# Loading each expert of the later groups of three in one transfer of 3 MiB, instead of two of 2 and 1 MiB

## The chip, the cores and the metric

The kernel runs on one core of one Trainium2 chip. The metric is the device time of one execution in microseconds (us). PE is the matrix engine, ACT the scalar engine, DVE the vector engine, POOL the general one, and SP the engine that only waits and issues DMA transfers here.

## What is computed

Two layers of a small diffusion transformer on 256 tokens of width 1024. Layer 0 mixes tokens by attention and a state space model, layer 1 by a long convolution (hyena). After the mixer each layer has a mixture of experts: 64 experts with a hidden width of 256, of which every token uses six, and a shared expert.

```python
def expert_block(args):
    toks, w, e = args
    xb = xf[toks]
    hid = jax.nn.silu(xb @ w_gate[e]) * (xb @ w_up[e])
    return (hid @ w_down[e]) * w[:, None].astype(xb.dtype)
...
routed = jnp.zeros_like(xf).at[row_tok].add(ys.reshape(n_rows, Dm))
shared = (jax.nn.silu(xf @ sh_gate) * (xf @ sh_up)) @ sh_down
return (routed + shared).reshape(B, L, Dm)
```

Everything is in 32-bit floats. One expert is 3 MiB: gate and up 2 MiB, down 1 MiB. All 64 are read in each layer, 192 MiB, whatever the routing.

## The kernel before

**Groups.** The 64 experts of a layer are worked through in 22 groups (`NG`). The first two are pairs, the other 20 are triples, numbered t = 0 to 19 (group n = t + 2). A triple puts its biggest expert in 64 rows of the array and the two others in 32 each. The order of the experts is computed at run time (`order`), so SP reads each expert's number into a register before it asks for its weights.

**The ring of weights.** On chip there are six slots of 3 MiB (`wring`, `RING = 6`), so triple t lies where triple t-2 lay. In memory an expert is one row per partition, gate and up (16 KiB) followed by down (8 KiB), and the slot has the same form. `half_loads` (L517) asks for one half of each expert of a triple, SP's queue having, for each t: three gate-and-up halves, each after a wait on `gu_mm` for group t-2 (its gate-and-up products are done), then three down halves, each after a wait on `dn_mm` for group t-2 (its down products are done). They count on `w_gu0` or `w_gu1`, and `w_dn0` or `w_dn1`, by the parity of t. All of these transfers are in one hardware queue and are served in order by the same 16 DMA engines.

**A group on PE** (`moe_pe`, the loop from L1091): wait for `w_gu` of its triple; gate-and-up products (64 matmuls of 512 columns); products that scatter the rows of the group before (`filler`), and those that pick and turn the rows of the group after; the turn of the hidden values; wait for `w_dn`; down products (32 matmuls), which count `dn_mm` up. `triple_loads(t, li)` is the number of expert loads that must have landed on one of the semaphores. In the trace all these matmuls have line 678, the turns of hidden values and of rows line 984, and every load has line 451. The last group has no next rows to pick and turn.

**After a stage.** When the last group is down, its rows are scattered, the residual is added, and layer 1's norm and projection follow on PE. The projection's weights (`hy_w_in`) are asked for after `dn_mm` of the last but one group.

Of the kernel before, what the change touches and what calls it, by code (L numbers as in the profile page):

```python
# [35 lines left out]
RING, FIRST_SLOT, SHARED = 6, 3, 2  # L36
# [3 lines left out]
PAIRS = STATIC // 2  # L40
NG = PAIRS + (NE - STATIC) // 3
BIG = STATIC + NG - PAIRS
FIRST, GROUP = 4, 12
SECOND, FILL_AT, LATER = 9, 11, 16
CTAB_STEPS = 24
# [54 lines left out]
def group_of(c):  # L100
    return c // 2 if c < STATIC else PAIRS + (c - STATIC) // 3
# [20 lines left out]
def program(nc, A):  # L122
# [8 lines left out]
    with ExitStack() as ctx:  # L131
        sems = {}

        def sem(name):
            if name not in sems:
                sems[name] = ctx.enter_context(nc.semaphore(name))
            return sems[name]
# [120 lines left out]
        wring = at(m1, RING * WEXP).rearrange("p (b n) -> p b n", b=RING)  # L258
# [40 lines left out]
        loads, ahead = rt_at(34, NE), rt_at(35, NE)  # L299
# [15 lines left out]
        def slot_of(e):  # L315
            return (e + FIRST_SLOT) % RING

        def triple_loads(t, li):

            fixed = li + 1 if t % 2 == 0 else 0  # L320
            return 3 * (li * len(range(t % 2, NG - PAIRS, 2)) + t // 2 + 1) - fixed
# [127 lines left out]
        def _(sp):  # L449
# [58 lines left out]
            def moe_loads(li):  # L508
                sp.wait_ge(sem("x_mixed"), KD * (li + 1))
                load(rw, A["router_w"][li], "rw_in")  # L510
                load(rt_at(0, NE), A["router_b"][li:li + 1].broadcast_to([P, NE]), "rw_in")
                load(at(r_mc, NMCST), A["mcst"], "rw_in")
                first_experts(li, (3, 4))

                def expert_at(c):
                    return sp.value_load(order[0:1, c:c + 1], min_val=0, max_val=NE - 1)
                GUW = 2 * KD * FF  # L517

                def half_loads(columns, experts, t, down):
                    part, name = (slice(GUW, WEXP), f"w_dn{t % 2}") if down else (slice(0, GUW), f"w_gu{t % 2}")  # L520
                    for c in columns:
                        if c - RING >= 0:
                            sp.wait_ge(sem("dn_mm" if down else "gu_mm"), li * NG + group_of(c - RING) + 1)
                        elif down:
                            sp.wait_ge(sem("sh_down"), li + 1)
                        else:
                            sp.wait_ge(sem("sh_gu"), 2 * (li + 1))
                        load(wring[:, slot_of(c), part], A["w_experts"][li, experts[c]][:, part], name)
                sp.wait_ge(sem("tables_ready"), TABLES * li + 1)
                first = {c: expert_at(c) for c in range(FIXED, STATIC + 6)}  # L530
                half_loads((5, 6), first, 0, False)
                half_loads((7,), first, 1, False)
                half_loads((5, 6), first, 0, True)
                half_loads((7,), first, 1, True)
                half_loads((8, 9), first, 1, False)
                half_loads((8, 9), first, 1, True)
                for t in range(2, NG - PAIRS):
                    triple = range(STATIC + 3 * t, STATIC + 3 * t + 3)
                    experts = {c: expert_at(c) for c in triple}
                    half_loads(triple, experts, t, False)  # L540
                    half_loads(triple, experts, t, True)
                if li == 0:
                    sp.wait_ge(sem("hscr_out"), 16)
                    sp.wait_ge(sem("dn_mm"), NG - 1)
                    for n in range(3):
                        load(hyw[:, n], A["hy_w_in"][HYP[n]], f"hyw_in{n}")
                sp.wait_ge(sem("dn_mm"), (li + 1) * NG)
                sp.wait_ge(sem("hscr_out"), 16 * (li + 1))

                def more(s, i):  # L550
                    sp.wait_ge(sem(f"ov_d{li}"), i * OVD + OVD * NE * (s - 1) + 1)
                    e = sp.value_load(order[0:1, bass.ds(i, 1)], min_val=0, max_val=NE - 1)
                    sp.dma_start(wring[:, 0], A["w_experts"][li, e]).then_inc(sem(f"ov_w{li}"), 16)
                overflow(li, sp, more)
# [121 lines left out]
        def _(pe):  # L676
# [55 lines left out]
            for i in range(FIRST):  # L732
                pe.wait_ge(sem(f"ada_c{i}"), 16)
                for k in range(KD):
                    g, a = k % 4, 2 * (GROUP - 1 - i)
                    last = mm(ps[32 * g:32 * g + 2 * GROUP, 4, :], scz[:, k, a:a + 2 * GROUP], ada_first[i][:, k],
                              i == 0 and k < 4, i == FIRST - 1 and k >= 4, skip=True)
                last.then_inc(sem("ada_mm"), 1)
            pe.wait_ge(sem("adrow_ready"), 1)
            for j in range(4):  # L740
                last = mm(ps[:, 3, 2 * FIRST * j:2 * FIRST * (j + 1)], adrow[:, j * P:(j + 1) * P], cst("fold")[:, 0:2 * FIRST], True, True)
# [3 lines left out]
            for k in range(KD):  # L745
                pe.wait_ge(sem("h_ctx"), k + 1)
                pe.wait_ge(sem("h_x"), k + 1)
                last = mm(ps[:, 0, :], w_in[:, k, QL:QL + KVL], hT[:, k], k == 0, k == KD - 1)
            last.then_inc(sem("proj_mm"), 1)
            for k in range(KD):  # L750
                g = k % 4
                last = mm(ps[32 * g:32 * g + ROPE, 1, :], w_in[:, k, QL + KVL:UOFF], hT[:, k], k < 4, k >= 4, skip=True)
            last.then_inc(sem("proj_mm"), 1)
            for i in range(2):
                for k in range(KD):
                    last = mm(ps[:, 2, i * L:(i + 1) * L], w_in[:, k, i * P:(i + 1) * P], hT[:, k, L:2 * L], k == 0, k == KD - 1)
# [16 lines left out]
            for i in range(2):  # L773
                last = mm(ps[:, 2, 0:L], ones, sql[0][:, i * L:(i + 1) * L], i == 0, i == 1)
# [11 lines left out]
            for h in range(HEADS):  # L786
                for k in range(2):
                    last = mm(ps[0:QKH, 3 + h // 2, (h % 2) * L:(h % 2 + 1) * L], w_uq[:, k, h * QKH:(h + 1) * QKH], ql[:, k], k == 0, k == 1)
# [30 lines left out]
            for h in (0, 2, 1, 3, 4, 6, 5, 7):  # L819
                if h % 4 == 0:  # L820
                    pe.wait_ge(sem("sq_head"), h // 2 + 2)
                last = head_sum(h, 0, L, sqq[:, h // 2, (h % 2) * L:(h % 2 + 1) * L], False)
# [20 lines left out]
            for h in (0, 2, 4, 6, 1, 3, 5, 7):  # L843
                last = over_features(ps[0:QKH, turning[h // 2], (h % 2) * L:(h % 2 + 1) * L], h, 2 * L, L, False)
# [79 lines left out]
            for n in range(2 * HEADS):  # L924
# [5 lines left out]
                for k in range(4):  # L930
                    last = pe.transpose(ps[:, 2 + n % 2, k * P:(k + 1) * P], prob[:, n % 3, k * P:(k + 1) * P], ident)  # L931
# [20 lines left out]
            for p in range(4):  # L952
                last = s5_outputs(p)
# [9 lines left out]
            for t in range(T5):  # L963
                last = pe.transpose(ps[:, 5 + t // 4, (t % 4) * P:(t % 4 + 1) * P], ys[:, t].rearrange("p g c -> p (g c)"), ident)  # L964
# [5 lines left out]
            for j in range(4):  # L970
                for k in range(4):
                    last = mm(ps[:, 5 + j // 2, (j % 2) * L:(j % 2 + 1) * L], glu_w[:, k, j * P:(j + 1) * P], zT[:, k], k == 0, k == 3)
# [8 lines left out]
            def moe_pe(li):  # L981
# [109 lines left out]
                for n in range(NG):  # L1091
                    t = n - PAIRS
                    if t < 0:
                        pe.wait_ge(sem(f"w_pair{n}"), 16 * (2, 3)[n] * (li + 1))
                    else:
                        pe.wait_ge(sem(f"w_gu{t % 2}"), 16 * triple_loads(t, li))
                    pe.wait_ge(sem("xt_act"), li * NG + n + 1)
                    pe.wait_ge(sem("xt_dve"), li * NG + n + 1)
                    if n >= 1:
                        pe.wait_ge(sem("h_done"), li * NG + n)  # L1100
                    gate_up_of(n).then_inc(sem("gu_mm"), 1)
                    if n == 0:
                        pe.wait_ge(sem("sh_hidden"), li + 1)
                    else:
                        pe.wait_ge(sem("oh_ready"), li * NG + n)
                        pe.wait_ge(sem("y_dve"), 2 * (li * NG + n))
                    filler(n, range(0, 4))
                    if n + 1 < NG:
                        pick_rows(n + 1)
                    filler(n, range(4, 6))  # L1110
                    if n < NSETS:
                        pe.wait_ge(sem("tables_ready"), TABLES * li + 2 + n)
                    pe.wait_ge(sem("h_done"), li * NG + n + 1)
                    for f in range(2):
                        last = turn(ps[:, HT, f * P:(f + 1) * P], hh[:, f * P:(f + 1) * P], ident, f == 0)
                    last.then_inc(sem("ht_mm"), 1)
                    if n + 1 < NG:
                        turn_rows(n + 1)
                    filler(n, range(6, KD)).then_inc(sem("sc_mm" if n >= 1 else "sh_down"), 1)
                    pe.wait_ge(sem("hT_ready"), li * NG + n + 1)  # L1120
                    if n + 1 < NG:
                        pe.wait_ge(sem("xt_act"), li * NG + n + 2)
                        pe.wait_ge(sem("xt_dve"), li * NG + n + 2)
                    if t >= 0:
                        pe.wait_ge(sem(f"w_dn{t % 2}"), 16 * triple_loads(t, li))
                    down_of(n).then_inc(sem("dn_mm"), 1)
                    if n + 1 < NSETS:
                        find_tokens(n + 1)
# [1117 lines left out]
```

## Time and profile before

| | us |
|---|---|
| median of three runs | 1501.29 |
| lowest and highest run | 1499.29, 1504.4 |
| the profiled execution's own time | 1497.9 |
| its span from first to last instruction | 1496.1 |
| PE busy | 1320.8 (88%) |
| expert stage of layer 0, from the first groups to the last down | about 320 to 786 |
| expert stage of layer 1 | about 1011 to 1479 |

The profile shows one execution. Its time is the span and 1.8 us around it. Section 1 of the page has the busy time of each engine, section 2 the same in 40 equal slices of 37.4 us with what the DMA engines moved, section 4 the chain of work that ended last (54% PE, 37% DMA), section 6 the transfers by size. A weight load that PE waits for ends a stretch of idle time; the timeline shows that time in brackets with what released it.

### The profile page before, as it was taken

The page shows a single profiled execution, that of the slowest core. Times are in us where ns is not written, and L with a number is a line of the kernel's source. Part 1 is how long each engine was busy: PE and PEld are TensorE (multiplying, and loading weights), DVE is VectorE, ACT ScalarE, POOL GpSimd, SP SyncE. Part 2 cuts the span into 40 slices and gives each one's busy share as a digit, 9 for nine tenths or more (in the row PEclk, how much of TensorE's full clock was granted, in tenths as well). Part 3 has the DMA queues.
Part 4 walks back from the last instruction along what each step waited for, and adds up shares of the span by engine and source line. Part 5 has one row for each costly group of instructions (what it writes and reads, how often), then busy time and mean ns, then how long its engine had stood idle before and what let it go on. Part 6 is the DMA issues. An engine that isn't in the chain of part 4 may idle for free.

```text
span 1496.1 us, 22046 instructions
## 1 busy us (share of the span) xinstructions
PE 1320.8 (88%) x9056; PEld 685.7 (46%) x9056; DVE 634.9 (42%) x1170; ACT 298.5 (20%) x501; POOL 66.7 (4%) x116
## 2 busy tenths in 40 slices
PE   4998778899998888897887999999999888898895
PEld 1444326764444333333436776875444333343342
DVE  5997733254433223222224788453433222322322
ACT  2236232311111111111112114031111111111110
POOL 0000681000000000000000000000000000000000
PEclk9999889999999999999997999989999999999998
DMA  9672963958999999999997870767999999999993
GB/s 381 238 180 71 188 262 126 396 219 322 420 423 421 423 423 423 423 423 423 422 423 230 303 297 29 303 245 267 380 424 424 421 425 421 421 424 423 422 423 130
DMA packets 59800, 502.79 MB, mean 336 GB/s; under 512 B 10348, under 2 KB 17260, under 8 KB 20588
## 3 DMA queue, kind: packets, MB, share of 16 engines
q1 hardware_dynamic: 59148, 499.19, 83.9%
q8 instruction: 76, 1.25, 0.3%
q10 hardware_dynamic: 544, 2.10, 0.3%
q14 instruction: 32, 0.26, 0.0%
HBM read 496.57 MB, written 4.69 MB: 335 GB/s over the span
## 4 chain that ended last, share of the span: by engine, by line
PE 54%; DMA 37%; DVE 4%; issue 2%; ACT 2%; SPq 1%; DVEq 0%; ACTq 0%
PE ps L678 50%; DMA arena<-in_w_experts 34%; DMA arena<-in_ada_w 3%; PE ps L407 2%; ACT arena L1278 1%; SPq L451 1%; PE ps L984 1%; DVE arena L1885 1%; PE ps L723 0%; ACT L1278 0%; DVE arena L1718 0%; PE ps L931 0%; DVE arena L1719 0%; DVE arena L1742 0%; DVE arena L1716 0%
## 5 line engine op out<-in xcount | busy, mean ns | idle before, releaser
L678 PE MATMUL ps<-arena 128*32 128x512 f32 (+12 forms) x8236 | 1235.1, 497 | 151.8 <-DMA arena<-in_w_experts 78.4
L678 PEld LDWEIGHTS ps<-arena 128*32 128x32 f32 (+6 forms) x8236 | 622.5, 132 | 749.2 <-issue 543.6
L1278 ACT ACTIVATE arena<-ps 128x512 f32<-128x512 f32 (+7 forms) x303 | 167.5, 553 | 928.9 <-PE ps L678 817.5
L1278 ACT ACTIVATE arena<-arena 128x256 f32<-128x256 f32 (+8 forms) x138 | 93.6, 700 | 171.5 <-DVE arena L1940 61.1
L1924 DVE SCALAR_TENSOR_TENSOR arena<-arena,ps 128x256 f32<-128x256 f32 x44 | 21.2, 481 | 234.1 <-ACT arena L1278 234.1
L1938 DVE CAST arena<-ps 128x512 bf16<-128x512 f32 x44 | 30.4, 692 | 175.0 <-PE ps L678 175.0
L1881 DVE COPY arena<-ps 128x512 f32<-128x512 f32 x44 | 30.4, 692 | 172.7 <-PE ps L678 172.7
L1914 DVE TENSOR_TENSOR arena<-arena 128x1024 bf16<-128x1024 f32 x44 | 53.9, 1226 | 39.5 <-ACT arena L1278 39.2
L1940 DVE TENSOR_TENSOR arena<-ps,arena 128x1024 f32<-128x1024 f32 x44 | 53.9, 1225 | 1.5
L668 POOL MEMSET arena<- 128x1 f32 x2 | 0.2, 101 | 1215.1 <-PE ps L984 1215.1
L984 PE MATMUL ps<-arena 128*128 128x128 f32 x352 | 52.8, 273 | 0.0
L407 PE MATMUL ps<-arena 128*24 128x512 f32 x256 | 35.6, 651 | 8.4 <-DMA arena<-in_ada_w 8.4
L1885 DVE COPY arena<-ps 128x512 f32<-128x512 f32 x44 | 30.4, 692 | 26.1 <-PE ps L984 26.1
L984 PEld LDWEIGHTS ps<-arena 128*128 128x128 f32 x352 | 41.4, 141 | 0.0
L1278 ACT ACT_TABLE_LOAD x15 | 19.2, 1283 | 67.7 <-PE ps L964 24.9
L1736 DVE TENSOR_REDUCE arena<-ps 128x1 f32<-128x512 f32 x16 | 11.1, 692 | 27.9 <-PE ps L678 27.7
L2055 DVE SCALAR_TENSOR_TENSOR arena<-arena 128x512 f32<-128x512 f32 x28 | 21.1, 752 | 1.2 <-DMA arena<-in_ada_w 0.3
L1932 DVE COPY arena<-ps 128x256 f32<-128x256 f32 x44 | 18.4, 419 | 5.2 <-PE ps L984 5.2
L1278 ACT ACTIVATE arena<-ps,arena 128x512 f32<-128x512 f32 (+3 forms) x29 | 17.0, 585 | 15.7 <-PE ps L678 14.9
L407 PEld LDWEIGHTS ps<-arena 128*24 128x24 f32 x256 | 6.1, 105 | 28.5 <-DMA arena<-in_ada_w 15.3
L931 PE MATMUL ps<-arena 128*128 128x128 f32 x64 | 10.7, 293 | 5.7 <-DVE arena L1742 5.7
L625 POOL TENSOR_TENSOR arena<-arena 128x64 f32<-128x64 f32 (+4 forms) x21 | 12.8, 608 | 60.3 <-ACT arena L1278 58.7
(225 smaller groups left out, 479.6 us busy)
## 6 DMA issues: line engine op xcount, KB each, us to landing
arena<-in_w_experts SPq DMA_DIRECT2D x118, 2048.0 KB, 28.0
arena<-in_w_experts SPq DMA_DIRECT2D x118, 1024.0 KB, 27.4
arena<-in_ada_w SPq DMA_DIRECT2D x40, 1024.0 KB, 6.5
arena<-in_w_experts SPq DMA_DIRECT2D x10, 3072.0 KB, 18.7
arena<-in_hy_w_in SPq DMA_DIRECT2D x6, 2048.0 KB, 12.0
arena<-in_ada_w SPq DMA_DIRECT2D x4, 2048.0 KB, 22.1
arena<-in_w_shared SPq DMA_DIRECT2D x2, 3072.0 KB, 10.5
arena<-in_hy_w_out SPq DMA_DIRECT2D x1, 4096.0 KB, 12.5
```

The source lines that it names most:

```text
L407: last = pe.matmul(ps[32 * k:32 * k + 2 * GROUP, 7, :], scz[:, 4 * half + k, a:a + 2 * GROUP], ada_half(i, half)[:, k], start=i == first a ...
L678: return pe.matmul(out, lhsT, rhs, start=start, stop=stop, skip_group_check=skip)
L984: return mm(out, in_, one, True, True) if first else pe.transpose(out, in_, one)
L1278: return act.activation(out, in_, func, **kw)
L1881: dve.tensor_copy(picked[:, 512:], ps[:, DN + 1, :]).then_inc(sem("picked_dve"), 1)
L1885: dve.tensor_copy(xgT[:, 4:8].rearrange("p k t -> p (k t)"), ps[:, DN + 1, :]).then_inc(sem("xt_dve"), 1)
L1914: tt(yb[:, 2], yr, yb[:, 1], SU).then_inc(sem("y_dve"), 1)
L1924: stt(hh, sg, wtab[:, n:n + 1], ps[:, GU, FF:2 * FF], M, M).then_inc(sem("h_done"), 1)
L1932: dve.tensor_copy(hT2.rearrange("p f t -> p (f t)"), ps[:, HT, 0:2 * P]).then_inc(sem("hT_ready"), 1)
L1938: ch(dve.tensor_copy(yb[:, 0, 0:512], ps[:, DN, :]))
L1940: tt(yr, ps[:, DN:DN + 2, :].rearrange("p b n -> p (b n)"), yb[:, 0], SU).then_inc(sem("y_dve"), 1)
L2055: ins = ts(ada_sums[n], w, c, None, M) if half == 0 and k == 0 else stt(ada_sums[n], w, c, ada_sums[n], M, AD)
```

## The change

`whole(t)` is true for t = 8 to 18. For such a triple SP waits, per expert, for the down products of group t-2, and then asks for all 3 MiB in one transfer, which counts on `w_gu`. PE waits for it ahead of gate-and-up, and no longer ahead of down. Triples 0 to 7 and 19 are loaded in halves as before. `down_loads` is the new count for `w_dn`. Nothing else differs.

```diff
+TRIPLES = NG - PAIRS
...
+        def whole(t):
+
+            return 8 <= t < TRIPLES - 1
+
+        def down_loads(t, li):
+
+            def loads(last):
+                return sum(0 if whole(i) else 2 if i == 0 else 3 for i in range(t % 2, last + 1, 2))
+            return li * loads(TRIPLES - 1) + loads(t)
+
...
                     experts = {c: expert_at(c) for c in triple}
+                    if whole(t):
+                        for c in triple:
+                            sp.wait_ge(sem("dn_mm"), li * NG + group_of(c - RING) + 1)
+                            load(wring[:, slot_of(c)], A["w_experts"][li, experts[c]], f"w_gu{t % 2}")
+                        continue
                     half_loads(triple, experts, t, False)
                     half_loads(triple, experts, t, True)
...
-                    if t >= 0:
-                        pe.wait_ge(sem(f"w_dn{t % 2}"), 16 * triple_loads(t, li))
+                    if t >= 0 and not whole(t):
+                        pe.wait_ge(sem(f"w_dn{t % 2}"), 16 * down_loads(t, li))
                     down_of(n).then_inc(sem("dn_mm"), 1)
```

## Rows read from the trace of the kernel before

**Rows 1.** The page's 40 slices: PE, DMA busy in tenths, GB/s.
```profile
PE   4998778899998888897887999999999888898895
...
DMA  9672963958999999999997870767999999999993
GB/s 381 238 180 71 188 262 126 396 219 322 420 423 421 423 423 423 423 423 423 422 423 230 303 297 29 303 245 267 380 424 424 421 425 421 421 424 423 422 423 130
```
**Rows 2.** Waits of PE, 460 to 780 us: us in total, times, longest.
```profile
PE ps L678 <- DMA arena<-in_w_experts: 39.6, 14, 4.9
```
**Rows 3.** PE timeline (start, us, what), the turn in two groups before DMA binds.
```profile
452.54 0.27 PE L984 MATMUL ps<-arena 128*128 128x128 f32 x1
...
471.01 0.27 PE L984 MATMUL ps<-arena 128*128 128x128 f32 x1
```
**Rows 4.** Windows: stretch, length, busy of each engine, clock, DMA share, GB/s.
```profile
500.00:740.00 240.00, 205.70 (x1497) 87.76 (x1490) 65.13 (x106) 34.65 (x54) 0.00 (x0) 0.96 1.01 423
...
948.00:972.00 24.00, 24.00 (x112) 20.96 (x112) 6.33 (x15) 1.62 (x4) 0.00 (x0) 1.00 1.00 429
```
**Rows 5.** PE timeline, the last three groups of layer 0 (t = 17 to 19).
```profile
727.74 12.82 PE L678 MATMUL ps<-arena 128*32 128x512 f32 x92 [2.06 <-DMA arena<-in_w_experts]
...
742.77 3.64 PE L678 MATMUL ps<-arena 128*32 128x512 f32 x32 [0.33 <-DVE arena L1885]
749.98 14.52 PE L678 MATMUL ps<-arena 128*32 128x512 f32 x92 [3.57 <-DMA arena<-in_w_experts]
...
766.71 3.64 PE L678 MATMUL ps<-arena 128*32 128x512 f32 x32 [0.33 <-DVE arena L1885]
772.23 9.39 PE L678 MATMUL ps<-arena 128*32 128x512 f32 x84 [1.89 <-DMA arena<-in_w_experts]
...
781.57 4.39 PE L678 MATMUL ps<-arena 128*128 128x256 bf16 x38
```
**Rows 6.** Windows of one gate-and-up each; the clock stands third from the end.
```profile
749.98:758.80 8.82, 8.82 (x65) 2.42 (x66) 1.05 (x2) 0.00 (x0) 0.00 (x0) 0.81 1.03 432
727.74:734.87 7.13, 7.13 (x65) 2.06 (x66) 1.49 (x2) 1.04 (x1) 0.00 (x0) 1.00 1.04 432
1171.37:1181.40 10.03, 10.03 (x66) 2.44 (x67) 1.49 (x2) 0.00 (x0) 0.00 (x0) 0.71 1.02 425
```
**Rows 7.** PE timeline, layer 1: t = 6, then t = 19.
```profile
1171.35 15.72 PE L678 MATMUL ps<-arena 128*32 128x512 f32 x92 [3.11 <-DMA arena<-in_w_experts]
...
1189.28 3.64 PE L678 MATMUL ps<-arena 128*32 128x512 f32 x32 [0.33 <-DVE arena L1885]
...
1463.66 11.08 PE L678 MATMUL ps<-arena 128*32 128x512 f32 x84 [4.08 <-DMA arena<-in_w_experts]
...
1474.69 4.39 PE L678 MATMUL ps<-arena 128*128 128x256 bf16 x38
```
**Rows 8.** The chain of waits: PE's end, then SP's first issue.
```profile
556.86 0.02 issue
...
557.02 0.34 SPq L451
```
**Rows 9.** SP's issue on an empty queue, and windows right after it.
```profile
944.93 0.33 SPq L451 DMA_DIRECT2D arena<-in_w_shared  x1
...
944.90:945.85 0.95, 0.95 (x6) 0.84 (x5) 0.88 (x3) 0.00 (x0) 0.00 (x0) 1.00 0.00 0
...
945.85:949.85 4.00, 4.00 (x20) 3.48 (x20) 3.72 (x9) 0.00 (x0) 0.00 (x0) 1.00 1.06 381
```
**Rows 10.** PE timeline, layer 0: t = 6, then t = 7 and 8.
```profile
480.13 14.52 PE L678 MATMUL ps<-arena 128*32 128x512 f32 x92 [3.11 <-DMA arena<-in_w_experts]
...
502.21 12.83 PE L678 MATMUL ps<-arena 128*32 128x512 f32 x92 [1.72 <-DMA arena<-in_w_experts]
...
517.25 3.64 PE L678 MATMUL ps<-arena 128*32 128x512 f32 x32 [0.33 <-DVE arena L1885]
525.79 4.64 PE L678 MATMUL ps<-arena 128*32 128x512 f32 x28 [4.90 <-DMA arena<-in_w_experts]
```

## The prediction

> **What bounds the kernel now.** I read the page's forty slices first [rows 1]. From the 11th slice to the 21st and from the 30th to the 39th, in the two expert stages, the DMA engines are busy throughout and move 420 to 425 GB/s; PE is busy for 80 to 90%. The reader is to see that the stream from memory doesn't pause, so it is the likely bound. PE's waits say the same: between 460 and 780 us PE waits 14 times for expert weights, 39.6 us in all [rows 2]. The PE timeline prices both sides. Unhindered, a group of three repeats every 18.5 us (452.54 to 471.01) [rows 3]. A triple of experts is 9 MiB = 9.44 MB, and 9.44 MB at the 423 GB/s of 500 to 740 us [rows 4] takes 22.3 us. Starts of gate-and-up 22.25 us apart (727.74, 749.98, 772.23) [rows 5] are exactly that. So from the seventh triple on (t = 6) DMA sets the pace, and PE idles 1.9 to 3.6 us a group.
>
> PE's own time from the start of gate-and-up to the end of down, W, has two common values: 727.74 to 746.41 = 18.7 us, and 749.98 to 770.35 = 20.4 us [rows 5]. The first gate-and-up ran at granted clock 1.00 in 7.13 us, the second at 0.81 in 8.82 us, a part of it at 1.2 GHz [rows 6]. The slower one follows the longer idle time (3.57 against 2.06 us). In layer 1 one took 10.03 us at 0.71 [rows 6]; W was 1171.35 to 1192.92 = 21.6 us [rows 7].
>
> **How much slack the order of requests leaves now.** Triple t takes the slots of t-2. Its gate-and-up halves (6 MiB) are asked for when gate-and-up of t-2 is through, its down halves (3 MiB) when down of t-2 is. PE starts t as soon as the gate-and-up halves land, 7.4 us (3.15 MB at 423) before the down halves do. The down request comes W = 20 us after that start, and the transfer is due 22.3 + 7.4 + 14.9 us after it; so the queue is tens of microseconds deep and never runs dry.
>
> **What the change does to it, for t = 8 to 18 (eleven triples, 33 experts a layer).**
>
> (a) Transfers. 66 transfers of 2 and 1 MiB become 33 of 3 MiB; the bytes are the same. SP issues 33 fewer at 0.33 us each, hidden under its waits. The pure 3 MiB stream at 948 to 972 us ran at 429 GB/s against 423 [rows 4]: 22.0 us a triple for 22.3, a gain of 0.31 us, times 11 = 3.4 us a layer. It counts only while the queue is continuous. I take it as measured; the bounds are 0 and twice that.
>
> (b) PE now needs all 9 MiB before gate-and-up. At t = 8 that shifts PE by 7.4 us relative to the stream, once; the bytes behind it aren't delayed. The shift costs nothing in the middle, as the stream sets the pace, but it must be repaid at the last triple. In layer 0 the halves of t = 19 landed at 772.2 [rows 5]. Their 6.29 MB take 14.9 us, so the down halves of t = 18 were in at 757.3. A whole t = 18 lands then, less the gain of (a): 753.9. PE runs it for W = 20.4 (it is an even one, which follow the long idle time) and reaches t = 19 at 774.3 instead of 772.2: +2.1 us. In layer 1: 1463.6 - 14.9 - 3.4 + 20.4 = 1465.7 against 1463.66 [rows 7]: +2.1 us. The last group then starts without idle time ahead of it. In layer 0 it took 772.23 to 785.96 = 13.7 us, in layer 1 1463.66 to 1479.08 = 15.4 [rows 5, 7], so layer 1 gets back 1.7. Sum of (a) and (b): +2.1 + 2.1 - 1.7 = **+2.5 us**. If W of t = 18 is 18.7 in both layers it is 3.4 less, -0.9. The new end of either layer is the PE chain that follows, so it passes on whole.
>
> (c) The moved request. The load of t+2 is asked for only at the end of down of t: start of t + W. Now start of t is the landing of the whole triple, and the stream has just t+1 left, 22.0 us. From the end of a group on PE to the start of SP's issue is 0.16 us (556.86 to 557.02) [rows 8]. An issue at 944.93 on an empty queue moved nothing before 945.85, and the next 4 us ran at 381 GB/s [rows 9] instead of 429, a loss of 0.45 us. The new transfer therefore runs at full value W + 0.16 + 0.95 + 0.45 = W + 1.55 us after the landing: 20.25, 21.95 or 23.15 us for the three W. Against 22.0: 1.75 us in hand, none, or 1.15 short. The cover that hid the request is gone in every second group.
> - t = 8 waits for its whole triple: in layer 0 from down's end at 520.9 [rows 10] to about 533 (the gate-and-up halves landed at 525.8, plus 7.4), 12 us idle. No row shows a group after so long an idle time; the nearest is the 21.6 of layer 1, and 18.7 is the other end. I take 21.6: t = 10 is 1.15 late.
> - Four more even groups are targets (t = 12 to 18). Their sources run slow, and the rows show both kinds, 8.8 and 10.0 us [rows 6]; the 8.8 has more rows. I count a third at 1.15 and two thirds at 0.1: 0.45 x 4 = 1.8 us.
> - The 16 DMA engines don't finish together. Now the interval of starts is 22.25 but now and then 23.6 (502.21 to 525.79) [rows 10]; the mean over t = 6 to 19 is (772.23 - 480.13)/13 = 22.47 [rows 5, 10]. A deep queue lets undisturbed engines run ahead; a shallow one doesn't, so a delay on any engine counts. Its price isn't shown; bounds 0 and, if the 0.22 doubles, 2.4 us a layer; I take 1.1, the middle, as nothing draws it to an end.
> Sum of (c): 1.15 + 1.8 + 1.1 = 4.05 a layer, **+8.1 us** (bounds 0 and 2 x (5 x 1.15 + 2.4) = 16.3).
>
> Nothing else is queued behind SP's moved wait: its next entries were the down requests with the same wait. PE loses eleven waits a layer on `w_dn`, none of which was ever last. The hyena weights of layer 1 are asked for after down of t = 18, at 774 instead of 770, while the stream is busy to about 776 with t = 19: hidden.
>
> **A rule that speaks for the change.** The measured gain per transfer removed is 0.31/3 = 0.1 us [rows 4]. The Trainium skill, "DMA: Bandwidth & Descriptors", section "Anatomy of one DMA", gives a fixed cost of about 2.0 us per DMA beside the movement. Charged to each of the 66 transfers saved, that would be an estimate of 132 us gained; the trace disagrees, since a queue with the next transfer waiting runs at 423 GB/s. The same fixed cost says what a dry queue pays, and there the trace has about 1.55 us.
>
> **Rivals.**
> 1. *Stall-free.* The queue stays continuous after all: W + 1.55 never exceeds what is left. For it: 21.95 against 22.0, and DMA engines that run behind have more left. Against: no margin. Time: 1497.9 + 2.5 = 1500.4, -0.9 to +4 around it; within 0.3%.
> 2. *Clock feedback, slower still.* A late landing lengthens PE's idle time, the next gate-and-up falls to 0.71 of the clock, W = 21.6 or more, and the next request is later. It decides as soon as idle time ahead of even groups passes some 4 us. For it: the 21.6 of layer 1 [rows 7]. Against: after 4.90 us idle at 525.8 W was 20.1. Time: the bound, 1497.9 + 2.5 + 16.3 = 1516.7.
> 3. *Faster.* The 3 MiB stream reaches 440 GB/s, as single slices of the trace do for a moment; 21.45 us a triple, gain 0.86 x 11 x 2 = 19 us instead of 6.8, 12 us more: 1488 if requests still kept up. But W + 1.1 = 21.5 already exceeds 21.45, so it can't be whole; with half the triples held at 22 half of the 12 us is left, 1494. (The Trainium skill's fixed cost above is this rival at its extreme.) Against it: 429 in the one row there is.
> 4. *Not what it says.* Before t = 8 the stream already sets the pace, so the change does bite; a semaphore count that made PE wait for t+2 would deadlock and not shift time. No chance of its own.
>
> **How the numbers follow.** Forecast: 1497.9 + 2.5 + 8.1 = 1508.5 us for an execution like the profiled one (span 1496.1 and 1.8 around it). That execution is 3.4 under the median of 1501.29, so for the median: 1501.3 + 10.6 = 1511.9 us. Chances: forecast 0.67, stall-free 0.22, feedback 0.07, faster 0.04. A measurement tells 0.3%, 4.5 us, from no change. The forecast's own low end (+5) lies just over that bound, so slower 0.73, same 0.23, faster 0.04. Range: from the stall-free case's low end, 1501.3 - 0.9 = 1500, to 1501.3 + 2.5 + 16.3 = 1520, and 3 more for the spread of the runs (1504.4 against 1501.3): 1523.
>
> **What would show it.** Step (a): GB/s of a stretch in t = 9 to 18, 429 if the queue is continuous. Step (b): t = 8 of each layer starts 12 us after the down before it; t = 19 starts with no idle time for DMA ahead of it, and the last group takes 13.7 us in both layers. Step (c): start intervals that alternate, about 22.0 and 22.3 to 23.1, DMA share under 1.00 in short windows after each whole landing, slow gate-and-ups in every second group. The prediction is wrong if intervals stay at 22.0 throughout (rival 1), or if PE's gate-and-up stays at 7.1 us, which would leave 1.75 us in hand everywhere.

## The result, and the profile after

The changed kernel takes 1523.45 us (median, 1522.54 to 1524.94) against 1500.29 us (the three runs of the table before and a fourth): a ratio of 1.0157, 95% interval 1.0136 to 1.0177, 23.2 us slower. The forecast had the sign and the mechanism, but less than half of the size, and the range ended 0.45 us short.

The page's slices, which answer to [rows 1], and its transfers by size (count, KB, median us to landing):

```profile
PE   4998778999999788888987999989999877898886
DMA  9572964958999999999996871767999999999993
GB/s 379 222 184 70 208 234 158 384 206 321 422 424 422 426 389 394 430 404 407 410 398 215 313 287 45 298 241 286 381 422 423 424 429 398 406 403 388 429 407 124
...
arena<-in_w_experts SPq DMA_DIRECT2D x76, 3072.0 KB, 19.1
arena<-in_w_experts SPq DMA_DIRECT2D x52, 2048.0 KB, 20.0
arena<-in_w_experts SPq DMA_DIRECT2D x52, 1024.0 KB, 18.8
...
arena<-in_w_shared SPq DMA_DIRECT2D x2, 3072.0 KB, 10.6
```

In the expert stage of layer 0 (11th to 21st slice) the stream is as before up to the 14th slice. From the 15th on, where the whole triples begin, it moves 389 to 410 GB/s, with one slice of 430; in layer 1, from the 34th slice on, it moves 388 to 407, with one of 429. So the stream now pauses. The last line matters below.

The PE timeline of layer 0 (start, us, what, the idle time before it and its releaser) from t = 8 to 13, and the end of the layer, which answer to [rows 5, 10]:

```profile
537.09 15.08 PE L694 MATMUL ps<-arena 128*32 128x512 f32 x92 [12.35 <-DMA arena<-in_w_experts]
559.05 12.83 PE L694 MATMUL ps<-arena 128*32 128x512 f32 x92 [1.14 <-DMA arena<-in_w_experts]
583.70 15.67 PE L694 MATMUL ps<-arena 128*32 128x512 f32 x92 [6.08 <-DMA arena<-in_w_experts]
601.46 3.64 PE L694 MATMUL ps<-arena 128*32 128x512 f32 x32 [0.22 <-DVE arena L1901]
605.77 12.82 PE L694 MATMUL ps<-arena 128*32 128x512 f32 x92 [0.66 <-DMA arena<-in_w_experts]
630.86 14.32 PE L694 MATMUL ps<-arena 128*32 128x512 f32 x92 [6.53 <-DMA arena<-in_w_experts]
653.04 3.27 PE L694 MATMUL ps<-arena 128*32 128x512 f32 x20 [2.12 <-DMA arena<-in_w_experts]
...
769.67 14.52 PE L694 MATMUL ps<-arena 128*32 128x512 f32 x92 [4.06 <-DMA arena<-in_w_experts]
786.29 12.83 PE L694 MATMUL ps<-arena 128*32 128x512 f32 x116 [0.22 <-DVE arena L1901]
799.07 4.39 PE L694 MATMUL ps<-arena 128*128 128x256 bf16 x38
```

t = 8 starts after 12.35 us idle, as foreseen. Then the distances between starts alternate: 21.96, 24.65, 22.07, 25.09, 22.18 us. At the end t = 19 begins in the same row as the down products of t = 18 (786.29, 116 matmuls), without idle time.

The whole difference by stage, from the starts of gate-and-up in the two timelines, in us:

| stage | layer 0: before, after | layer 1: before, after | sum of differences |
|---|---|---|---|
| t = 7 to t = 8 | 23.6, 31.0 | 22.2, 29.5 | +14.7 |
| t = 8 to t = 18 | 224.2, 232.6 | 225.1, 233.4 | +16.7 |
| t = 18 to t = 19 | 22.3, 20.1 | 22.8, 18.4 | -6.6 |
| last group | 13.7, 13.7 | 15.4, 13.7 | -1.7 |

That is 23.1 us, the difference of the medians. The two profiled executions (1497.9 and 1524.0) are 3 us further apart, and that part lies outside the stages.

**One dry restart**, end of down of t = 10 (605.10) to the start of t = 12. SP's row, then windows with clock, DMA share and GB/s at the end:

```profile
605.30 1.37 SPq L462 DMA_DIRECT2D arena<-in_w_experts  x3
```

```profile
603.00:604.00 1.00, 1.00 (x12) 0.31 (x8) 0.00 (x0) 0.00 (x0) 0.00 (x0) 1.00 0.24 98
604.00:605.00 1.00, 1.00 (x12) 0.16 (x4) 0.00 (x0) 0.00 (x0) 0.00 (x0) 1.00 0.12 49
605.00:606.20 1.20, 0.54 (x8) 0.16 (x8) 1.00 (x2) 0.60 (x1) 0.00 (x0) 1.00 0.00 0
606.30:608.30 2.00, 2.00 (x24) 0.57 (x20) 0.88 (x2) 1.06 (x1) 0.00 (x0) 1.00 1.06 332
608.30:610.30 2.00, 2.00 (x24) 0.64 (x20) 1.43 (x2) 0.00 (x0) 0.00 (x0) 1.00 0.91 393
610.30:626.00 15.70, 13.81 (x100) 6.65 (x92) 4.27 (x8) 2.18 (x4) 0.00 (x0) 1.00 1.00 430
```

A window counts a packet of 24 KB, 0.9 us long, where it starts, so after 603 few DMA engines begin another (0.24, then 0.12). By the packets in the trace 12 of the 16 have done their part of t = 11 by 603.9, the last at 605.3, and its landing is seen at 605.7, when PE starts it (605.77). SP asks at 605.30; nothing moves before 606.2; full rate is back after 610. t = 12 starts at 630.86, which is 25.8 us after the end of down. 9.44 MB at 430 GB/s are 21.95, so this restart costs 3.8 us beside the bytes. The same span is there at every even triple, t = 10 to 18 in both layers: 25.6 to 26.4 us, mean 26.0, so a restart costs 4.0 us on average. For instance in layer 1, down of t = 14 to the start of t = 16, and of t = 16 to t = 18:

```profile
1396.88 3.64 PE L694 MATMUL ps<-arena 128*32 128x512 f32 x32 [0.22 <-DVE arena L1901]
...
1426.47 14.17 PE L694 MATMUL ps<-arena 128*32 128x512 f32 x92 [6.84 <-DMA arena<-in_w_experts]
...
1442.73 3.64 PE L694 MATMUL ps<-arena 128*32 128x512 f32 x32 [0.22 <-DVE arena L1901]
...
1472.17 12.83 PE L694 MATMUL ps<-arena 128*32 128x512 f32 x92 [3.35 <-DMA arena<-in_w_experts]
```

1400.52 to 1426.47 is 25.95, 1446.37 to 1472.17 is 25.8. So the rule with which I went into the experiments (theory A; I took the span as 25.9): on a chain of triples two apart, start to start takes W + 25.9 us if the queue ran dry, and the pair can't be faster than the stream's 43.9. It is dry once W exceeds 18.0. W of the even groups was 19.8 to 21.6, mean 20.6.

### The profile page after: what moved, and what is told of

Same layout as the page of the kernel before. It is cut to its first block, busy times and chain, and to the rows that moved or that the text cites. A ratio compares the mean times of both kernels' runs of the same rounds, so it can differ in the third digit from the quotient of the medians.

```text
span 1522.1 us, 21826 instructions
## 1 busy us (share of the span) xinstructions
PE 1326.7 (87%) x9056; PEld 687.7 (45%) x9056; DVE 635.6 (42%) x1170; ACT 298.6 (20%) x501; POOL 66.8 (4%) x116
## 4 chain that ended last, share of the span: by engine, by line
PE 63%; DMA 28%; DVE 5%; issue 2%; ACT 1%; SPq 1%; DVEq 0%; ACTq 0%
PE ps L694 58%; DMA arena<-in_w_experts 24%; DMA arena<-in_ada_w 3%; PE ps L418 2%; PE ps L1000 2%; SPq L462 1%; DVE arena L1901 1%; ACT arena L1294 1%; PE ps L947 0%; PE ps L739 0%; DVE arena L1734 0%; DMA arena<-in_mcst 0%; DVE arena L1735 0%; ACT L1294 0%; DVE arena L1732 0%
## 5 line engine op out<-in xcount | busy, mean ns | idle before, releaser
L1000 PEld LDWEIGHTS ps<-arena 128*128 128x128 f32 x352 | 41.4, 141 | 0.0
L1948 DVE COPY arena<-ps 128x256 f32<-128x256 f32 x44 | 18.4, 419 | 5.3 <-PE ps L1000 5.3
L418 PEld LDWEIGHTS ps<-arena 128*24 128x24 f32 x256 | 6.4, 106 | 26.4 <-issue 13.9
L947 PEld LDWEIGHTS ps<-arena 128*128 128x128 f32 x64 | 8.2, 151 | 16.1 <-DVE arena L1758 11.0
## 6 DMA issues: line engine op xcount, KB each, us to landing
arena<-in_hy_w_in SPq DMA_DIRECT2D x6, 2048.0 KB, 10.1
arena<-in_ada_w SPq DMA_DIRECT2D x4, 2048.0 KB, 22.2
```

The source lines that it names most:

```text
L418: last = pe.matmul(ps[32 * k:32 * k + 2 * GROUP, 7, :], scz[:, 4 * half + k, a:a + 2 * GROUP], ada_half(i, half)[:, k], start=i == first a ...
L1000: return mm(out, in_, one, True, True) if first else pe.transpose(out, in_, one)
```

## The experiments

Each runs beside the kernel before, whose median was 1498.4 to 1499.6 us. "Halves" are the transfers of 2 and 1 MiB.

**1. Late requests alone** (in the kernel before):

```diff
-                            sp.wait_ge(sem("dn_mm" if down else "gu_mm"), ...)
+                            sp.wait_ge(sem("dn_mm" if down or 8 <= t < 19 else "gu_mm"), ...)
```

> Halves of 2 and 1 MiB as in the kernel before, PE's waits as before; only the gate-and-up halves of t = 8 to 18 are asked for after the down products of t-2 too. Theory A (a late request hurts only together with PE's late start, because then the queue holds no more than one triple, 22 us, while the request comes W = 18.6 to 20.4 us after the start and takes nearly 4 us to be at full rate): here PE starts 7.4 us earlier than the queue's backlog ends, about 29.7 us are queued, so no stall: within 2 us of the kernel before, start intervals 22.25. Rival B (any request made only after the down products stalls the stream): 12 us or more slower.

Measured: 1499.98 us, ratio 1.0019 (1.0002 to 1.0035), +1.6 us. The starts stay 22.25 us apart:

```profile
593.34 12.83 PE L678 MATMUL ps<-arena 128*32 128x512 f32 x92 [1.88 <-DMA arena<-in_w_experts]
615.58 14.52 PE L678 MATMUL ps<-arena 128*32 128x512 f32 x92 [3.57 <-DMA arena<-in_w_experts]
637.84 12.83 PE L678 MATMUL ps<-arena 128*32 128x512 f32 x92 [1.88 <-DMA arena<-in_w_experts]
```

The late request by itself costs next to nothing: rival B, with 12 us or more, falls.

**2. PE waits for the whole triple, requests as before:**

```diff
+                    if 8 <= t < 19:
+                        pe.wait_ge(sem(f"w_dn{t % 2}"), 16 * triple_loads(t, li))
                     gate_up_of(n).then_inc(sem("gu_mm"), 1)
```

> Transfers and requests exactly as in the kernel before; only PE waits, for t = 8 to 18, for the down halves too before it starts gate-and-up. Theory A: the stream never runs dry, intervals stay at 22.25; only the 7.4 us shift has to be repaid at t = 19: about 5.5 us in layer 0 and 3.8 in layer 1, together +8 to +10 us over the kernel before. Rival C (PE's wait for the whole triple is the cost by itself): +20 us or more.

Measured: 1509.40 us, ratio 1.0079 (1.0049 to 1.0110), +11 us. The stream doesn't pause (window of 560 to 740 us, GB/s last), and in the PE timeline behind it t = 19 starts within the row at 776.26, straight after t = 18:

```profile
560.00:740.00 180.00, 155.31 (x1129) 70.36 (x1124) 48.98 (x81) 25.87 (x40) 0.00 (x0) 0.95 1.01 423
```

```profile
759.54 14.52 PE L678 MATMUL ps<-arena 128*32 128x512 f32 x92 [3.57 <-DMA arena<-in_w_experts]
...
776.26 12.82 PE L678 MATMUL ps<-arena 128*32 128x512 f32 x116 [0.33 <-DVE arena L1887]
```

So the shift of 7.4 us is paid at the end of each layer and nowhere else (from t = 8 to t = 18 the two layers take 224.1 and 225.4 us, as in the kernel before), and the cost is a little more than the 8 to 10 expected. Rival C falls as the main cause.

**3. Both at once, still in halves** (the edits of 1 and 2):

> Both at once, still in halves of 2 and 1 MiB: late requests and PE waiting for all. Theory A: the stalls of the changed kernel without its faster stream: every second interval 24 to 25.5 us, the others 22.3, in all some 5 to 8 us slower than the changed kernel, so about +30 us over the kernel before. Rival D (the 3 MiB transfers are what costs): well under the changed kernel, +10 us over the kernel before.

Measured: 1539.58 us, ratio 1.0280 (1.0250 to 1.0310), +41 us, 11 more than I expected. Its profiled execution was 1531.3, +33; the spread between them stays unexplained. The alternation is there without a single whole transfer:

```profile
625.00 15.22 PE L678 MATMUL ps<-arena 128*32 128x512 f32 x92 [6.35 <-DMA arena<-in_w_experts]
642.42 3.64 PE L678 MATMUL ps<-arena 128*32 128x512 f32 x32 [0.33 <-DVE arena L1887]
647.23 12.82 PE L678 MATMUL ps<-arena 128*32 128x512 f32 x92 [1.17 <-DMA arena<-in_w_experts]
...
672.72 2.79 PE L678 MATMUL ps<-arena 128*32 128x512 f32 x12 [6.82 <-DMA arena<-in_w_experts]
```

646.06 to 672.72 is 26.7 us; less 22.3 for the bytes at 423 GB/s it is 4.4. That is the longest of the ten even spans of this run; they are 26.2 to 26.7, mean 26.4, which leaves 4.1: the same restart as with whole transfers. +1.6 and +11 make +41 together: the loss is an interaction. The 3 MiB transfers aren't its cause (rival D falls). With them the loss is 23 us, and their denser stream accounts for at most some 7 us of the difference.

**4 and 5. The clock's share.** Idle matmuls into a bank that is about to be overwritten, four after the odd whole triples, then two after each:

```diff
                     down_of(n).then_inc(sem("dn_mm"), 1)
+                    if whole(t) and t % 2 == 1:
+                        for _ in range(4):
+                            mm(ps[:, GU, :], ident, at(r_cst, 512), True, True)
```

> The changed kernel with four idle matmuls of 128x512 after the down products of t = 9, 11, 13, 15 and 17, into a bank that the next gate-and-up overwrites: they fill the idle time ahead of the even triples, so that these start at full clock. Theory A with a share of the clock: W of the even triples 18.6 instead of 20.3 to 21.4, their requests that much earlier, the even intervals from t = 12 on down from 24.4 to about 22.6: 12 to 16 us faster than the changed kernel. Rival (the clock only follows the stall and doesn't feed it): no faster than the changed kernel.

> The changed kernel with two idle matmuls of 128x512, 1.8 us, after the down products of every whole triple, instead of four after the odd ones. Theory A: idle time ahead of a group is about 2 us on both chains, both run at full clock, W = 18.6, a pair takes 44.5 us instead of 46.3: 8 to 10 us a layer less stall, the time 14 to 18 us under the changed kernel, some 6 over the kernel before. Rival (the clock's share is small): within 4 us of the changed kernel.

Measured: 1521.06 us (ratio 1.0143, 1.0107 to 1.0180) and 1526.06 (1.0197, 1.0165 to 1.0228), so neither gave what I expected. Windows of the gate-and-up of t = 10 and of t = 11 in the first, clock third from the end:

```profile
580.61:587.74 7.13, 7.13 (x65) 2.08 (x66) 0.00 (x0) 0.00 (x0) 0.00 (x0) 1.00 1.01 430
602.57:611.40 8.83, 8.83 (x66) 2.41 (x67) 1.22 (x2) 0.00 (x0) 0.00 (x0) 0.81 1.02 436
```

The even triple now runs at full clock, but the odd one, after 3.4 us idle, has taken over the lower clock, and then the four matmuls (3.6 us) delay the even start further: the time went from one chain to the other. With two matmuls after each, 5.5 us gaps stayed partly open and the lower clock came back in most even groups. Where it didn't, in layer 0 from t = 14 on, the pair from 674.44 to 719.12 took 44.7 us, as W + 25.9 = 44.5 says, but the next, from 719.12 to 764.76, took 45.6, which the rule doesn't explain. How much of the 23 us the clock carries isn't settled by these two.

**6 and 7. Leaner groups.** 15 of 24 scatter matmuls left out (`ks = ks[:1]` in `filler` for t = 8 to 18), in both kernels:

> The kernel before with 15 of the 24 scatter matmuls of rows left out in the groups t = 8 to 18 (their routed rows are missing from the result): W is about 3.1 us shorter, 15.6 or 17.3 us. The stream sets the pace, so intervals stay at 22.25 and the time at that of the kernel before, within 3 us. It is the partner of the next run.

> The changed kernel with the same 15 scatter matmuls left out. Theory A, as it stands now: two chains, of the even and of the odd triples, each W + 25.9 us from one start to the next but one (25.9 = from the end of down to the landing of 9.44 MB on a dry queue), so a pair of groups takes the larger of that and 43.9, the stream. With W at most 17.3 that is 43.9: the stalls are gone, intervals about 22.0 throughout, and the time is within 3 us of the light kernel before instead of 23 over it. Rival (each 3 MiB request costs some fixed time wherever it is made): still some 20 us over its partner.

Measured: 1500.96 (1.0005, 0.9992 to 1.0019) and 1517.92 us (1.0123, 1.0083 to 1.0162), 17 us apart. W fell by 1 us only at full clock (17.6 for 18.6), since PE then waits for the engines beside it (0.55 where it was 0.22), and after the long idle times the lower clock is still there, so that W of the even groups has a mean of 19.9:

```profile
581.13 13.64 PE L694 MATMUL ps<-arena 128*32 128x512 f32 x80 [6.56 <-DMA arena<-in_w_experts]
597.19 3.64 PE L694 MATMUL ps<-arena 128*32 128x512 f32 x32 [0.55 <-DVE arena L1903]
...
626.84 12.97 PE L694 MATMUL ps<-arena 128*32 128x512 f32 x80 [5.72 <-DMA arena<-in_w_experts]
```

600.83 - 581.13 = 19.7, over the 18.0 of the rule. The expectation of no stall rested on a W that wasn't reached, so these two runs don't test the threshold. They do bear out the rule above it: 581.13 to 626.84 is 45.7 us, for W + 25.9 = 45.6, and the ten even spans have the same mean of 26.0.

**8 and 9. Half of gate-and-up left out** (four of eight blocks of the width, t = 8 to 18), in both kernels:

```diff
+                    ks = range(KD // 2 if 8 <= n - PAIRS < 19 else KD)
-                    for k in range(KD):
+                    for k in ks:
```

> The kernel before with half of the gate-and-up matmuls (the last four blocks of the width) left out in the groups t = 8 to 18, so the routed experts' values are incomplete there. W falls by about 3.5 us to 15.1, or some 17 at the lower clock. The stream sets the pace: intervals 22.25, time within 3 us of the kernel before. Partner of the next run.

> The changed kernel with the same half of the gate-and-up matmuls left out. Theory A: a triple lands W + 25.9 us after the start of the one two before it if its queue was dry, else by the stream's 43.9. With W of 15 to 17 the first is 41 to 43, so the queue isn't dry: intervals 22.0 throughout from t = 9 on, no odd-even pattern, and the time within 3 us of its partner, or a little under it. The leaner scatter of the earlier pair left W at 17.6 to 20.5, above the 18.0 at which the rule turns, and so proved nothing of the threshold. Rival (each 3 MiB request has a fixed cost wherever it is made): even intervals of 24 remain and the time is 15 to 20 us over its partner.

Measured: 1502.10 us (1.0024, 1.0009 to 1.0039) and 1497.15 us (0.9990, 0.9975 to 1.0004). With the same cut the changed kernel is 5 us *faster* than its partner. Its PE timeline, and the window from 560 to 740 us:

```profile
601.61 10.98 PE L694 MATMUL ps<-arena 128*32 128x512 f32 x60 [4.51 <-DMA arena<-in_w_experts]
614.69 3.64 PE L694 MATMUL ps<-arena 128*32 128x512 f32 x32 [0.22 <-DVE arena L1902]
624.15 11.66 PE L694 MATMUL ps<-arena 128*32 128x512 f32 x60 [5.82 <-DMA arena<-in_w_experts]
637.89 3.64 PE L694 MATMUL ps<-arena 128*32 128x512 f32 x32 [0.22 <-DVE arena L1902]
646.12 10.92 PE L694 MATMUL ps<-arena 128*32 128x512 f32 x60 [4.58 <-DMA arena<-in_w_experts]
...
668.08 11.87 PE L694 MATMUL ps<-arena 128*32 128x512 f32 x60 [5.32 <-DMA arena<-in_w_experts]
```

```profile
560.00:740.00 180.00, 137.91 (x888) 59.77 (x880) 48.77 (x80) 25.85 (x40) 0.00 (x0) 0.88 1.00 426
```

W is 16.7 (601.61 to 618.33) and 17.4 (624.15 to 641.53), below 18.0; the intervals are 22.5, 22.0 and 22.0; no pattern. (Single intervals elsewhere reach 23.2 after the jump at t = 8; its partner has some of 23.6.) This is the decisive run: the lower clock is still there (0.88 over the stretch) and idle gaps are 5 us, and neither costs anything as long as W and the restart of 4.0 stay under the stream's 22 us. Whole transfers as such cost nothing here.

**10. One whole triple, t = 8** (`return t == 8`):

> The changed kernel with only t = 8 loaded whole. Theory A: PE starts t = 8 7.4 us late and catches up within three groups out of its spare time, the requests behind it being as early as before: within 2 us of the kernel before. Rival (the jump at the first whole triple is itself a loss): +7 us a layer, +14.

Measured: 1500.51 us, ratio 0.9998 (0.9978 to 1.0018). As expected, the jump at the first whole triple costs nothing by itself: in the trace t = 9 and 10 start without idle time and t = 11 waits for DMA again.

**11. Every third triple whole** (`return t in (7, 10, 13, 16)`):

> The changed kernel with only t = 7, 10, 13 and 16 whole. Theory A: each whole triple starts 7.4 us late, PE catches up in the two groups between, no two whole triples share slots two apart, so no request is late and the last triple isn't touched; only the denser stream is left, 0.3 us x 4 x 2 = 2.4 us faster than the kernel before, which is hardly measurable (0.998, within 0.3%). Rival (whole triples cost wherever they stand): four twentieths of the changed kernel's loss or more, +8 us.

Measured: 1496.35 us, ratio 0.9983 (0.9969 to 0.9998), 2.3 us faster than the kernel before, for 2.4 expected. Its window from 560 to 740 us, and the PE timeline at the start of t = 13 and of t = 19:

```profile
560.00:740.00 180.00, 147.62 (x1096) 66.94 (x1091) 47.30 (x78) 24.81 (x40) 0.00 (x0) 0.92 1.01 424
```

```profile
649.77 14.31 PE L694 MATMUL ps<-arena 128*32 128x512 f32 x92 [8.69 <-DMA arena<-in_w_experts]
...
777.02 9.39 PE L694 MATMUL ps<-arena 128*32 128x512 f32 x84 [2.14 <-DMA arena<-in_w_experts]
```

PE idles 8.7 us ahead of a whole triple and has caught up by the next, and before t = 19 there is idle time for DMA again, so nothing is left to repay. It beats both kernels, by an amount at the edge of what can be measured.

## Why the prediction was right or wrong

**What bounds the kernel**: right. Light kernels ran no faster (experiments 6 and 8).

**(a) The denser stream**: right in sign, and its size is shown only roughly. 0.31 us a triple gives 2.4 us in experiment 11, measured 2.3, but the interval is 0.3 to 4.6. In experiment 9, with eleven whole triples a layer, the median is 5 us under its partner's; in the profiled executions the stretches from t = 8 to 18 are 3.5 us shorter together, where 0.31 a triple gives 6.2, since that stream moved 426 GB/s over 180 us and not 429.

**(b) The shift and its repayment**: right in kind. t = 8 came 7.5 and 7.2 us later, and the last groups got back 2.2, 4.4 and 1.7. The net is 6.4 us for 9.3 foreseen (2.5 and the 6.8 of the gain); in layer 1 t = 18 ran at full clock, W = 18.6 instead of the 20.4 I had taken. Experiment 2 shows it alone, at 11 us.

**(c) The moved request**: the failed step, and in it one term. I priced the way from the end of down to full rate at 0.16 + 0.95 + 0.45 = 1.55 us, and took that for the whole delay of the landing; the delay is 4.0. That puts the point of decision at W = 18.0 instead of 20.45, so that *every* even group is late, not one in three, by 2.4 us on average: the even intervals are 24.4 us, ten of them, 24.2 us over the stream's 22.0. Odd intervals add 1.7, and the 3.1 us by which the old intervals exceeded 22.3 are gone. That makes (c) 22.8 us for 8.1 foreseen. With the -6.2 of (a), taken as foreseen, and the 6.4 of (b) it is 23.0, the 23.1 of the table but for rounding.

The missing 2.4 us is in the trace of before, in a row that I didn't read: the time from issue to landing of the shared expert, 3 MiB. The page has the median of two, and the tile's view both:

```profile
arena<-in_w_shared SPq DMA_DIRECT2D x2, 3072.0 KB, 10.5
...
DMA to landing us min/median/max: 10.0/10.5/11.0
```

The one of 11.0 us is the issue at 944.93 on the empty queue [rows 9]. 3.15 MB at 429 GB/s take 7.3 us; 3.7 us are fixed, and with the 0.16 ahead of the issue that is 3.9. I had instead added up the start of the transfer from windows of GB/s, which see when the first bytes move and when the sum of 16 engines is at its rate, but not when the last engine is done, and PE waits for the last. In the restart above 0.2 us go to the request, 0.9 to the first byte, 0.6 to the low rate up to 610.3 (98 and 37 GB/s missing over 2 us each); the other 2.1, found by subtraction, lie at the end, where the engines of one transfer finish one after the other. In the trace the 16 landings of that triple's last transfer run from 629.1 to 630.8: 13 of them within 0.4 us, two 0.4 later and the last 0.9 after those. That spread is 1.7 us; the other 0.4 is about the time between an engine's last packet and its landing (605.28 and 605.72 for t = 11).

The Trainium skill, "DMA: Bandwidth & Descriptors", section "Anatomy of one DMA", puts the fixed cost at about 2.0 us for a transfer issued from GpSimd; these are issued from SP. By it, as an estimate, the point of decision would have been W = 20.0, and most even groups late by little. The measured 4.0 decides; a dry queue does pay a fixed cost, and its use as a gain per transfer saved was rightly refused.

**Rivals.** Stall-free fell: intervals alternate. Faster fell: the continuous stream ran at 430, as in the row before. Clock feedback was half right: W of the even groups had a mean of 20.6, about what I took for them, so the clock wasn't mis-sized; but with the right price of a restart that W costs more. It didn't run away: the idle time ahead of t = 10 to 18 was mostly past the 4 us of this rival (3.4 to 6.8), and W stayed at 21.6 or less. Its share alone stays open (experiments 4 and 5). The price for uneven engines (1.1 us a layer) was about right as far as it can be told: the odd intervals, with means of 22.1 and 22.2 us, add 0.7 and 1.1 us to the stream's 22.0, in layer 1 nearly all of it in one interval of 23.2 (t = 8 to 9). What share it has in the even ones isn't shown.

**The range** took its upper end from the same 1.55 us and was too narrow by that.

## What to carry to other kernels

Two waits that cost 1.6 and 11 us alone cost 41 together: count how much work is in the DMA queue at the moment of the next request, and compare it with the time to the request plus a whole restart. Take the price of a restart from a transfer that ran on an empty queue, issue to landing less its bytes at the stream's rate, and not from when the first bytes move. A larger transfer into a ring has to wait for the last reader of its slot and hold up the first, so use it where a missed start can be caught up (every third triple here), and not in the last groups.

## What the runs showed of the hardware

- A stream of 3 MiB transfers moved 429 to 431 GB/s in stretches of 16 to 24 us and 426 over 180 us (experiment 9); one of 2 and 1 MiB moved 423, if the queue never emptied.
- A restart of the empty queue cost 4.0 us beside the bytes with 3 MiB transfers and 4.1 with halves (means of ten); in the one taken apart, half of its 3.8 us is at the end, where the engines finish apart.
- A PE idle time of 3.4 us or more was often followed by a gate-and-up of 8.4 to 10.1 us, in part at 1.2 GHz, where 7.13 is full clock; so were some of 2.1 us (8.8 us at t = 13 of layer 0). Kept warm in one group, it turned up in the next.
